# Turning the inverse's first matrices on VectorE instead of TensorE, with GpSimd taking a copy and half a low part per head turn

## The chip, the core and the metric

The kernel runs on one core of a Trainium2 chip. The metric is the device time of one execution in microseconds; lower is better. The core's engines run at the same time and meet only at semaphores: PE (TensorE) multiplies and loads weights, DVE (VectorE), ACT (ScalarE) and POOL (GpSimd) work elementwise, SP issues the loads from memory.

## What is computed

Two transformer blocks over 256 tokens of width 1024. The second holds a hybrid mixer of 8 heads: an HGRN2 part and a gated delta rule part. Cut to what the change touches:

```python
def gated_delta_chunked(q, k, v, beta, g):
    gam = jnp.cumsum(g, axis=-1)
    Lmat = jnp.exp(jnp.where(incl, gam[..., :, None] - gam[..., None, :], -jnp.inf))
    kb = k * beta[..., None]
    A = jnp.where(strict, jnp.einsum('bhntk,bhnsk->bhnts', kb, k) * Lmat, 0.0)
    T = lax.linalg.triangular_solve(eye + A, eye, left_side=True, lower=True, unit_diagonal=True)
    u = jnp.matmul(T, v * beta[..., None])
    w = jnp.matmul(T, kb * jnp.exp(gam)[..., None])
    ...
```

T is the inverse of a unit lower triangular matrix. The kernel builds it by doubling: the inverses of the 2x2 diagonal blocks, then of 4x4, and so on up to 128x128. It needs each intermediate both as it is (`yi`, `yc`) and turned (`xi`, `xc`).

## The kernel before

All projections go through weight chunks of 128x2048 numbers (1 MB). A ring of three slots holds each chunk three times: as loaded (`w_raw`), its rounded high part (`w_hi`, written by ACT in `split`), and the rest, the low part (`w_lo`, written by DVE: `w_low`, `w_low_half`, both through `low_of`, L1241). PE multiplies the high and the low parts (L2102 to L2109, L2114, L2121). SP loads the next chunk into a slot once its low part is written (`slot_free` waits on `lo_ready`).

The stage in question is a loop over the heads: `head(0)`, then seven turns of a loop, then `head(GH)`. Turn i does the projections of head i (24 quarters, six chunks) and, spread between them, the scans and the inverse of head i-1. Each engine's order is written out by hand, in its own `head`; semaphores tie them together. The loop's last six turns repeat one another.

At the end of a turn, for the head just projected:

- DVE writes unit matrices into `yi` (L1977, four 128x128 matrices side by side), later the first level: `nt` is the scaled negative of A (L2004), and a masked copy (L2007) puts its entries next to the diagonal into `yi`. A drain then raises `y0_ready`.
- PE, between quarters 21 and 22, turns the four matrices of `yi` through the unit matrix (L3004) into PSUM and raises `t_done`.
- ACT copies them to `xi` (L1193, `t_ready`) and two quadrants into `xc` (L1195).
- DVE meanwhile writes the low part of the next turn's first chunk in two halves (L1241), then scans (L2014), writes `hk` (L2015, `qk_ready`), takes the differences of the first two scan levels (`middle(1)`, `middle(2)`: L1796, `dd_ready`), `mt` (L2020), the scores (L2024, `lt2_ready`), empties a projection (L2028), and writes the gated output's low part (`delta_out_low`, L1740, `ogl_ready`).

At the start of the next turn PE asks in order for `t_ready`, `ntc_ready` and `lt2_ready` (first product of level 1, `inv_z(1)`, L2849), for the first chunk's low part (L2798), for `ogl_ready` (`inv_w(1)`, L2867), and for `xx_ready` (`inv_z(2)`, L2849 again). DVE gives `xx_ready` with a masked copy (`inverse(1)`, L1840) behind four small products (L1810, L1811) and one half of a low part.

Before the change POOL builds masks at the start, writes one whole low part (L631) and is otherwise idle.

Of the kernel before, what the change touches and what calls it, by code (L numbers as in the profile page):

```python
# [83 lines left out]
def emit(nc, ctx, a, out):  # L84
# [3 lines left out]
    def sem(name):  # L88
        return ctx.enter_context(nc.semaphore(name))
# [189 lines left out]
    def quad(ap, side):  # L279
        return ap[HD * side:HD * side + HD, :, :, HD * side:HD * side + HD].rearrange("p i e c -> p (i e) c")  # L280

    def kept(ap, side):
        return ap[HD * side:HD * side + HD, :, :, :].rearrange("p i e c -> p (i e) c")
# [4 lines left out]
    def yh_bank(tile):  # L288
        if tile < 4:
# [15 lines left out]
    w_loaded = [sem(f"w_loaded{s}") for s in range(RING)]  # L305
    slot_passed = sem("slot_passed")
    waited = sem("waited")
# [44 lines left out]
                         "gbc_ready", "gam_done", "lt_pre", "lt_ready"))  # L352
    qk_done, y0_ready, t_done, t_ready, ffn_step = (
        sem(n) for n in ("qk_done", "y0_ready", "t_done", "t_ready", "ffn_step"))
    zz_done, zc_ready, ww_done, wt_done, xx_ready, yy_ready, yt_done, xc_ready, ntc_ready = (
# [5 lines left out]
        sem(n) for n in ("gsq_ready", "gss_done", "grs_ready", "ogh_ready", "ogl_ready"))  # L361

    gate_tanh = sem("gate_tanh")
    ohh_ready, ohl_ready, ym_ready, ymh_ready, yml_ready = (
# [33 lines left out]
    def _(sp):  # L398
        def slot_free(c):
            if isinstance(c, int) and c < RING:  # L400
                return
            sp.wait_ge(lo_ready, c - RING + 1)
            sp.sem_inc(slot_passed, 1)

# [164 lines left out]
    def _(pool):  # L569
# [55 lines left out]
        for l in range(LEVELS):  # L625
# [5 lines left out]
        nc.gpsimd.tensor_tensor(w_lo[:, slot, :], w_raw[:, slot, :], w_hi[:, slot, :].bitcast(F32), ALU.subtract  # L631
                                ).then_inc(lo_ready, 1)

    BUILT_ID = 3
# [5 lines left out]
    def _(act):  # L640
# [303 lines left out]
        def head(i, gemm, main):  # L944
# [241 lines left out]
            if gemm:  # L1186
                act.wait_ge(y0_ready, i + 1)
                for side in range(2):
                    ins = nc.scalar.activation(kept(ntc, side), quad(nt, side), ACT.Copy)
                ins.then_inc(ntc_ready, 1)  # L1190
                act.wait_ge(t_done, i + 1)
                x0 = M[:, 5, :].rearrange("p (i e c) -> p i e c", i=TT, e=2)
                nc.scalar.activation(xi, x0, ACT.Copy).then_inc(t_ready, 1)  # L1193
                for side in range(2):
                    ins = nc.scalar.activation(kept(xc, side), quad(x0, side), ACT.Copy)  # L1195
                ins.then_inc(xc_ready, 1)
                level_exp(1, i + 1)
                level_exp(2, i + 1)
                nc.scalar.activation(n21, nt[:, :, :, HD:P], ACT.Copy)
# [34 lines left out]
    def _(dve):  # L1234
# [532 lines left out]
        def head(i, gemm, main):  # L1767
# [19 lines left out]
            def middle(l):  # L1787
                if l > 2 and not main:
                    return
                if l == 8:  # L1790
                    v.tensor_tensor(dd[:, 0, 0:P], hb[:, 0:P], hb[:, P - 1:P].to_broadcast([P, P]), ALU.subtract
                                    ).then_inc(dd_ready, 1)
                    return
                sz = 1 << (l - 1)
                blocks = hb.rearrange("p (n s) -> p n s", s=2 * sz)
                v.tensor_tensor(dd[:, l % 2, :].rearrange("p (n s) -> p n s", s=2 * sz), blocks,  # L1796
                                blocks[:, :, sz - 1:sz].to_broadcast([P, P // sz, 2 * sz]), ALU.subtract).then_inc(dd_ready, 1)

# [176 lines left out]
            if gemm:  # L1975
                key_lengths()
                v.tensor_copy(yi, ident[:].unsqueeze(1).unsqueeze(1).to_broadcast([P, TT, 2, P]))  # L1977
            w_low_j(2)
# [16 lines left out]
            if gemm:  # L1995
# [6 lines left out]
                for e in range(2):  # L2002
                    for b in range(TT):
                        v.scalar_tensor_tensor(out=nt[:, b, e, :], in0=kk[:, 2 * b, :], scalar=nbst[:, b, e:e + 1],  # L2004
                                               in1=lt[:, e, 2 * P * b:2 * P * b + P], op0=ALU.mult, op1=ALU.mult)
                settle()
                v.copy_predicated(yi, lmask[:, 0, :].bitcast(I32).unsqueeze(1).unsqueeze(1).to_broadcast([P, TT, 2, P]), nt)  # L2007
                v.drain().then_inc(y0_ready, 1)
                if main:
                    w_low_half(c0 + 3 + RING, 0, i, 6)  # L2010
                    w_low_half(c0 + 3 + RING, 1, i, 6)
                dve.wait_ge(lnf_ready, i + 1)
# [14 lines left out]
                dve.wait_ge(tok_done, i + 1)  # L2027
                v.tensor_copy(tok[:, 0, :], G[:, 1, :]).then_inc(evac[1], 1)  # L2028
                if main:
                    delta_out_low(i)  # L2030
                else:
                    w_low(c0 + 3 + RING, i, 6)
            settle()
# [61 lines left out]
    def _(pe):  # L2095
# [662 lines left out]
        def head(i, gemm, main):  # L2758
# [239 lines left out]
            quarter(21)  # L2998
            if gemm:
                pe.wait_ge(y0_ready, i + 1)  # L3000
                for b in range(TT):
                    for e in range(2):
                        at = T * b + P * e
                        ins = nc.tensor.transpose(M[:, 5, at:at + P], yi[:, b, e, :], ident[:])  # L3004
                ins.then_inc(t_done, 1)
            quarter(22)
# [81 lines left out]
```

## Time and profile before

| | |
|---|---|
| median of 3 runs | 1360.8 us (1360.49 to 1361.06) |
| the profiled execution | 1361.01 us, of which the trace's span is 1359.3 us |
| PE, share of the span busy | 99% |
| PE weight loads | 89% |
| DVE | 77% |
| ACT | 59% |
| POOL | 2% |
| granted TensorE clock, mean | 0.999 |
| one of the six like turns of the head loop | 49.26 us |

A row of a timeline gives the start of an instruction (or of a run of like ones), how long it took, its engine, line, operation and tiles, and in brackets how long the engine was idle before it and what released it, where that shows. Consecutive instructions overlap: the distance from start to start is what one costs its engine, and the duration is somewhat longer. Nearly all small tiles lie in one buffer and are called `arena`.

### The profile page before, as it was taken

How to read it: one execution, taken by the hardware profiler on the slowest of the kernel's cores; microseconds unless marked ns; L12 is line 12 of the kernel's file. 1: busy time of each engine (PE TensorE's matmuls, PEld its weight loads, DVE VectorE, ACT ScalarE, POOL GpSimd, SP SyncE). 2: the span in 40 equal slices, each digit the busy share in tenths (PEclk: the TensorE clock that was granted, in tenths of full speed). 3: DMA queues.
4: the chain of work that ended last, by engine and by line, in shares of the span. 5: the costliest groups of instructions: out<-in, count | busy, mean ns of one | idle time of the engine just before them, and what ended most of it. 6: DMA issues, size and time to landing. Idle time of an engine off the chain costs nothing.

```text
span 1359.3 us, 24392 instructions
## 1 busy us (share of the span) xinstructions
PE 1345.3 (99%) x8590; PEld 1208.7 (89%) x8590; DVE 1043.2 (77%) x1644; ACT 797.4 (59%) x1352; POOL 28.9 (2%) x72
## 2 busy tenths in 40 slices
PE   8999999999999999999999999999999999999998
PEld 7888888989888888888899999999999998988887
DVE  5798888777666686666778898888898877666665
ACT  4445555644344364444668898898898853544444
POOL 6000000000000010000000000000000000000000
PEclk9999999999999999999999999999999999999999
DMA  8565545655555756666574444554544286566661
GB/s 267 155 195 156 157 124 173 200 194 198 186 186 191 230 150 203 186 185 186 155 187 133 132 125 129 139 147 114 147 131 123 87 211 203 173 206 198 192 186 62
DMA packets 291215, 227.80 MB, mean 168 GB/s; under 512 B 10883, under 2 KB 270165, under 8 KB 291157
## 3 DMA queue, kind: packets, MB, share of 16 engines
q1 hardware_dynamic: 291012, 226.75, 56.2%
q8 instruction: 38, 0.62, 0.2%
q10 hardware_dynamic: 144, 0.26, 0.1%
q14 instruction: 21, 0.16, 0.0%
HBM read 225.90 MB, written 1.08 MB: 167 GB/s over the span
## 4 chain that ended last, share of the span: by engine, by line
PE 93%; DVE 3%; ACT 2%; issue 1%; DVEq 0%; ACTq 0%; DMA 0%
PE G L2114 11%; PE M L2114 10%; PE M L2107 7%; PE M L2108 7%; PE M L2109 7%; PE G L2121 6%; PE G L2102 5%; PE M L2121 5%; PE G L2104 5%; PE G L2103 5%; PE G L2264 2%; PE M L2867 1%; PE M L2849 1%; PE G L2107 1%; PE G L2109 1%; PE G L2108 1%
## 5 line engine op out<-in xcount | busy, mean ns | idle before, releaser
L1241 DVE TENSOR_TENSOR w_lo<-w_raw,w_hi 128x2048 fp32r<-128x2048 f32 (+2 forms) x247 | 477.7, 1942 | 122.1 <-ACT w_hi L655 114.9
L655 ACT ACTIVATE w_hi<-w_raw 128x2048 fp32r<-128x2048 f32 x197 | 375.9, 1909 | 171.4 <-PE M L2121 35.2
L2102 PE MATMUL G<-xa,w_hi 128*128 128x256 f32 x592 | 176.9, 299 | 0.0
L2104 PE MATMUL G<-xa,w_lo 128*128 128x256 f32 x592 | 167.2, 283 | 0.0
L2103 PE MATMUL G<-xa,w_hi 128*128 128x256 f32 x592 | 167.0, 282 | 0.0
L2114 PE MATMUL M<-xa,w_hi 128*128 128x512 f32 x600 | 147.9, 391 | 0.0
L2114 PE MATMUL G<-xa,w_hi 128*128 128x512 f32 x568 | 141.2, 392 | 0.0
L2114 PEld LDWEIGHTS M<-xa,w_hi 128*128 128x128 f32 x600 | 111.4, 188 | 23.0
L2114 PEld LDWEIGHTS G<-xa,w_hi 128*128 128x128 f32 x568 | 104.5, 188 | 21.0 <-issue 0.5
L2107 PE MATMUL M<-w_hi,xb 128*128 128x512 f32 x300 | 117.1, 390 | 0.1
L2108 PE MATMUL M<-w_lo,xb 128*128 128x512 f32 x300 | 116.9, 390 | 0.0
L2109 PE MATMUL M<-w_hi,xb 128*128 128x512 f32 x300 | 116.7, 389 | 0.0
L2102 PEld LDWEIGHTS G<-xa,w_hi 128*128 128x128 f32 x592 | 112.9, 191 | 1.4 <-issue 1.3
L2103 PEld LDWEIGHTS G<-xa,w_hi 128*128 128x128 f32 x592 | 112.9, 191 | 0.0
L2104 PEld LDWEIGHTS G<-xa,w_lo 128*128 128x128 f32 x592 | 112.6, 190 | 0.0
L882 ACT ACTIVATE arena<-arena 128x256 f32<-128x256 f32 x38 | 15.9, 418 | 137.4 <-DVE arena L1658 137.4
L2121 PE MATMUL M<-xa,w_lo 128*128 128x256 f32 x600 | 83.6, 284 | 0.0
L2121 PEld LDWEIGHTS G<-xa,w_lo 128*128 128x128 f32 x568 | 75.7, 191 | 3.8
L2121 PE MATMUL G<-xa,w_lo 128*128 128x256 f32 x568 | 78.4, 282 | 0.0
L2121 PEld LDWEIGHTS M<-xa,w_lo 128*128 128x128 f32 x600 | 76.9, 192 | 0.3
L2109 PEld LDWEIGHTS M<-w_hi,xb 128*128 128x128 f32 x300 | 56.3, 188 | 11.9
L2107 PEld LDWEIGHTS M<-w_hi,xb 128*128 128x128 f32 x300 | 56.4, 188 | 11.7 <-issue 0.4
(467 smaller groups left out, 2537.7 us busy)
## 6 DMA issues: line engine op xcount, KB each, us to landing
w_raw<-in_w_in SPq DMA_DIRECT2D x150, 512.0 KB, 4.9
w_raw<-in_ffn_w_in SPq DMA_DIRECT2D x88, 512.0 KB, 5.0
w_raw<-in_w_ff SPq DMA_DIRECT2D x64, 512.0 KB, 4.2
w_raw<-in_ffn_w_out SPq DMA_DIRECT2D x44, 512.0 KB, 4.9
w_raw<-in_w_in SPq DMA_DIRECT2D x33, 256.0 KB, 3.2
w_raw<-in_w_out SPq DMA_DIRECT2D x16, 512.0 KB, 3.8
w_raw<-in_w_branch_gdn SPq DMA_DIRECT2D x16, 512.0 KB, 5.3
w_raw<-in_w_branch SPq DMA_DIRECT2D x12, 512.0 KB, 4.5
```

The lines of the kernel that those rows point to most:

```text
L655: nc.scalar.activation(w_hi[:, slot, :], w_raw[:, slot, :], ACT.Copy).then_inc(hi_ready, 1)
L882: nc.scalar.activation(ffn_s[:, n, :], ffn_s[:, n, :], ACT.Silu).then_inc(ffr_ready, 1)
L1241: return v.tensor_tensor(dst, src, hi.bitcast(F32), ALU.subtract)
L2102: mm(out_, w[0], x[0], start=first, stop=False)
L2103: mm(out_, w[0], x[1], start=False, stop=False)
L2104: return mm(out_, w[1], x[0], start=False, stop=last_)
L2107: mm(out_, x[0], w[0], start=first, stop=False)
L2108: mm(out_, x[0], w[1], start=False, stop=False)
L2109: return mm(out_, x[1], w[0], start=False, stop=last_)
L2114: ins = mm(bank.rearrange("p (h t) -> p h t", h=2), wh[:, k, :], x[:, :, k, :], start=first and k == 0, stop=last_ and k == n - 1, skip_gr ...
L2121: ins = mm(bank[:, 0:T], wl[:, k, :], x[:, 0, k, :], start=first and k == 0, stop=last_ and k == n - 1, skip_group_check=first)
L2264: ins = mm(G[:, j, CW * i:CW * i + CW], x[:, k, P * i:P * i + P], w[j][:, k, :], start=first and k == 0, stop=last and k == KT - 1)
```

## The change

DVE turns the first matrices itself: `v.transpose` turns each 32x32 block of `yi` in its place and writes `xi`. At this level `yi` holds entries only in the 2x2 blocks on the diagonal, so this is the whole matrix turned. PE's four turns and `t_done` go, and so does ACT's copy from PSUM; ACT's quadrant copies read `xi`.

In the loop, the unit matrices are written by POOL, after `vn1_done` (the last product that reads the old `yi`), and DVE waits for them (`yi_ready`) ahead of its masked copy. POOL writes the first half of the low part of the next turn's first chunk, after `hi_ready` and `qk_ready`. DVE writes the second half, now behind L2028 and a wait for POOL's half (`pool_low`), and only this raises `lo_ready`. In `head(0)` it replaces a whole low part at that place. The differences of scan levels 1 and 2 become a scalar_tensor_tensor with the same two tensor inputs. SP's semaphore for passed slots is merged with another.

```diff
@@ gpsimd @@
+        c = FIRST["heads"] + 3 + RING
+        slot = c % RING
+        def first_half_low():
+            part = slice(0, CHUNK // 2)
+            nc.gpsimd.tensor_tensor(w_lo[:, slot, part], w_raw[:, slot, part], w_hi[:, slot, part].bitcast(F32), ALU.subtract
+                                    ).then_inc(pool_low, 1)
+        pool.wait_ge(hi_ready, c + 1)
+        pool.wait_ge(qk_ready, 1)
+        first_half_low()
+        with pool.Fori(1, GH) as i:
+            pool.wait_ge(vn1_done, i)
+            pool.sem_inc(waited, 1)
+            nc.gpsimd.tensor_copy(yi, ident[:].unsqueeze(1).unsqueeze(1).to_broadcast([P, TT, 2, P])).then_inc(yi_ready, 1)
+            pool.wait_ge(hi_ready, c + 1 + i * 6)
+            pool.wait_ge(qk_ready, i + 1)
+            pool.sem_inc(waited, 1)
+            first_half_low()
@@ scalar @@
-                act.wait_ge(t_done, i + 1)
-                x0 = M[:, 5, :].rearrange("p (i e c) -> p i e c", i=TT, e=2)
-                nc.scalar.activation(xi, x0, ACT.Copy).then_inc(t_ready, 1)
+                act.wait_ge(t_ready, i + 1)
                 for side in range(2):
-                    ins = nc.scalar.activation(kept(xc, side), quad(x0, side), ACT.Copy)
+                    ins = nc.scalar.activation(kept(xc, side), quad(xi, side), ACT.Copy)
@@ vector @@
+                if l <= 2:
+                    v.scalar_tensor_tensor(out=out_, in0=blocks, scalar=1.0, in1=middles, op0=ALU.mult, op1=ALU.subtract
+                                           ).then_inc(dd_ready, 1)
+                    return
+                v.tensor_tensor(out_, blocks, middles, ALU.subtract).then_inc(dd_ready, 1)
...
-                v.tensor_copy(yi, ident[:].unsqueeze(1).unsqueeze(1).to_broadcast([P, TT, 2, P]))
+                if not main:
+                    v.tensor_copy(yi, ident[:].unsqueeze(1).unsqueeze(1).to_broadcast([P, TT, 2, P]))
...
+                if main:
+                    dve.wait_ge(yi_ready, i)
+                    dve.sem_inc(waited, 1)
                 v.copy_predicated(yi, lmask[:, 0, :].bitcast(I32).unsqueeze(1).unsqueeze(1).to_broadcast([P, TT, 2, P]), nt)
                 v.drain().then_inc(y0_ready, 1)
-                if main:
-                    w_low_half(c0 + 3 + RING, 0, i, 6)
-                    w_low_half(c0 + 3 + RING, 1, i, 6)
+                v.transpose(xi.rearrange("p i e c -> p (i e c)"), yi.rearrange("p i e c -> p (i e c)")).then_inc(t_ready, 1)
...
                 v.tensor_copy(tok[:, 0, :], G[:, 1, :]).then_inc(evac[1], 1)
+                dve.wait_ge(pool_low, i + 1)
+                w_low_half(c0 + 3 + RING, 1, i, 6)
                 if main:
                     delta_out_low(i)
-                else:
-                    w_low(c0 + 3 + RING, i, 6)
@@ tensor @@
-            if gemm:
-                pe.wait_ge(y0_ready, i + 1)
-                for b in range(TT):
-                    for e in range(2):
-                        at = T * b + P * e
-                        ins = nc.tensor.transpose(M[:, 5, at:at + P], yi[:, b, e, :], ident[:])
-                ins.then_inc(t_done, 1)
```

How DVE's instructions stand at the end of a loop turn, before. `M` and `G` are the two PSUM tensors, `xb` holds the gated output.

```order
552 L2007 COPY_PREDICATED arena<-masks,arena 128x512
553 L1252 REGISTER_ALU
554 L1241 TENSOR_TENSOR w_lo<-w_raw,w_hi 128x1024 [waits hi_ready] x2
555 L2014 SCALAR_TENSOR_TENSOR arena<-ones,arena 128x128 [waits lnf_ready]
556 L2014 SCALAR_TENSOR_TENSOR arena<-ones,arena 128x128
558 L2015 SCALAR_TENSOR_TENSOR arena<-arena 128x256
559 L1796 TENSOR_TENSOR arena<-arena 128x256 x2
560 L2020 TENSOR_TENSOR arena<-M,arena 128x256
561 L2024 SCALAR_TENSOR_TENSOR arena<-M,arena 128x384 [waits qk_done]
563 L2028 COPY arena<-G 128x512 [waits tok_done]
566 L1740 SCALAR_TENSOR_TENSOR xb<-M,arena,xb 128x512
```

And the same stretch of the changed kernel, whose line numbers are higher by 18 to 27:

```order
552 L2034 COPY_PREDICATED arena<-masks,arena 128x512 [waits yi_ready]
553 L2036 STREAM_TRANSPOSE arena<-arena 128x512
554 L2039 SCALAR_TENSOR_TENSOR arena<-ones,arena 128x128 [waits lnf_ready]
557 L2040 SCALAR_TENSOR_TENSOR arena<-arena 128x256
558 L1817 SCALAR_TENSOR_TENSOR arena<-arena 128x256 x2
559 L2045 TENSOR_TENSOR arena<-M,arena 128x256
560 L2049 SCALAR_TENSOR_TENSOR arena<-M,arena 128x384 [waits qk_done]
562 L2053 COPY arena<-G 128x512 [waits tok_done]
563 L1270 REGISTER_ALU [waits pool_low]
564 L1259 TENSOR_TENSOR w_lo<-w_raw,w_hi 128x1024 [waits hi_ready]
567 L1758 SCALAR_TENSOR_TENSOR xb<-M,arena,xb 128x512
```

The two halves of the low part ahead of the scan have become one transposition; one half stands behind L2053 now, ahead of L1758.

PE's instructions between quarters 21 and 22 in the loop, before:

```order
2293 L2108 MATMUL G<-w_lo,xa 128x512
2294 L2109 MATMUL G<-w_hi,xa 128x512
2295 L3004 MATMUL M<-ident,arena 128x128 [waits y0_ready]
2296 L3004 MATMUL M<-ident,arena 128x128 x3
2297 L2107 MATMUL M<-w_hi,xa 128x512
```

And now:

```order
2291 L2133 MATMUL G<-w_lo,xa 128x512
2292 L2134 MATMUL G<-w_hi,xa 128x512
2293 L2132 MATMUL M<-w_hi,xa 128x512
2294 L2133 MATMUL M<-w_lo,xa 128x512
```

The four turns and their wait for `y0_ready` have gone; the two quarters follow each other directly.

## Rows read from the trace of the kernel before

**Rows 1.** The page: busy time and share of the span by engine.

```profile
PE 1345.3 (99%) x8590; PEld 1208.7 (89%) x8590; DVE 1043.2 (77%) x1644; ACT 797.4 (59%) x1352; POOL 28.9 (2%) x72
```

**Rows 2.** Timeline of PE at a turn's end: start, duration, engine, line.

```profile
813.90 0.39 PE L2109 MATMUL G<-w_hi,xa 128*128 128x512 f32 x1
814.13 0.60 PE L3004 MATMUL M<-ident,arena 128*128 128x128 f32 x4
...
814.80 0.39 PE L2108 MATMUL M<-w_lo,xa 128*128 128x512 f32 x1
```

**Rows 3.** Timeline of PE and its weight loads, the next turn's start (L2849 twice).

```profile
817.32 0.62 PE L2849 MATMUL M<-arena 128*128 128x128 f32 x4
...
818.95 0.64 PE L2798 MATMUL G<-xa,w_lo 128*128 128x256 f32 x4
...
821.63 0.54 PEld L2849 LDWEIGHTS M<-arena 128*128 128x128 f32 x4
821.74 0.62 PE L2849 MATMUL M<-arena 128*128 128x128 f32 x4
```

**Rows 4.** Timeline of DVE over the same boundary.

```profile
810.44 0.74 DVE L2007 COPY_PREDICATED arena<-masks,arena 128x512 f32<-128x512 int32 x1
811.38 2.36 DVE L1241 TENSOR_TENSOR w_lo<-w_raw,w_hi 128x1024 fp32r<-128x1024 f32 x2 [0.20 <-issue]
813.66 0.73 DVE L2014 TENSOR_TENSOR_SCAN arena<-ones,arena 128x128 f32<-128x128 f32 x2
814.31 0.46 DVE L2015 SCALAR_TENSOR_TENSOR arena<-arena 128x256 f32<-128x256 f32 x1
814.86 0.76 DVE L1796 TENSOR_TENSOR arena<-arena 128x256 f32<-128x256 f32 x2
816.04 1.02 DVE L2024 SCALAR_TENSOR_TENSOR arena<-M,arena 128x384 f32<-128x384 f32 x2
816.98 0.68 DVE L2028 COPY arena<-G 128x512 f32<-128x512 f32 x1
817.57 0.74 DVE L1740 SCALAR_TENSOR_TENSOR xb<-M,arena,xb 128x512 f32 x1
820.83 0.74 DVE L1840 COPY_PREDICATED arena<-masks,M 128x256 f32<-128x256 int32 x1
```

**Rows 5.** Timelines of ACT and SP over the same boundary.

```profile
811.24 0.60 ACT L1173 ACTIVATE arena<-arena 128x256 f32<-128x256 f32 x1 [0.21 <-issue]
...
828.48 1.90 ACT L655 ACTIVATE w_hi<-w_raw 128x2048 fp32r<-128x2048 f32 x1
```

```profile
813.99 0.37 SPq L413 DMA_DIRECT2D w_raw<-in_w_in  x1
```

**Rows 6.** Timelines of DVE and POOL while POOL writes its one low part.

```profile
480.49 1.23 DVE L1690 TENSOR_TENSOR arena<-res,arena 128x1024 f32<-128x1024 f32 x1
481.63 0.68 DVE L1493 SCALAR_TENSOR_TENSOR res<-res,M 128x512 f32<-128x512 f32 x1
485.84 0.89 DVE L1500 SCALAR_TENSOR_TENSOR arena<-res,stat,arena 128x512 f32<-128x512 f32 x1
490.62 0.75 DVE L1609 SCALAR_TENSOR_TENSOR arena<-res,stat,arena 128x512 f32<-128x512 f32 x1 [0.54 <-ACT stat L864]
```

```profile
480.61 5.57 POOL L631 TENSOR_TENSOR w_lo<-w_raw,w_hi 128x2048 fp32r<-128x2048 f32 x1 [454.40 <-ACT w_hi L655]
```

**Rows 7.** Timelines of POOL and DVE while the masks are built.

```profile
18.33 2.17 POOL L622 TENSOR_SCALAR_AFFINE_SELECT masks<-masks 128x64 f32<-128x64 f32 x1
23.84 0.24 POOL L622 TENSOR_SCALAR_AFFINE_SELECT masks<-masks 128x64 f32<-128x64 f32 x1
```

```profile
18.01 2.37 DVE L1241 TENSOR_TENSOR w_lo<-w_raw,w_hi 128x2048 fp32r<-128x2048 f32 x1 [0.68 <-ACT w_hi L655]
```

**Rows 8.** Timelines of PE and DVE at the first boundary and the last.

```profile
720.12 0.75 PE L2798 MATMUL G<-xa,w_lo 128*128 128x256 f32 x4 [0.54 <-DVE w_lo L1241]
```

```profile
1066.72 0.74 DVE L1840 COPY_PREDICATED arena<-masks,M 128x256 f32<-128x256 int32 x1 [0.36 <-PE M L2867]
```

More of the change, by code:

```diff
@@ L305, in emit @@
     w_loaded = [sem(f"w_loaded{s}") for s in range(RING)]
-    slot_passed = sem("slot_passed")
     waited = sem("waited")
@@ L352, in emit @@
                          "gbc_ready", "gam_done", "lt_pre", "lt_ready"))
-    qk_done, y0_ready, t_done, t_ready, ffn_step = (
-        sem(n) for n in ("qk_done", "y0_ready", "t_done", "t_ready", "ffn_step"))
+    qk_done, y0_ready, t_ready, ffn_step = (
+        sem(n) for n in ("qk_done", "y0_ready", "t_ready", "ffn_step"))
     zz_done, zc_ready, ww_done, wt_done, xx_ready, yy_ready, yt_done, xc_ready, ntc_ready = (
@@ L361, in emit @@
         sem(n) for n in ("gsq_ready", "gss_done", "grs_ready", "ogh_ready", "ogl_ready"))
+    yi_ready, pool_low = sem("yi_ready"), sem("pool_low")
     gate_tanh = sem("gate_tanh")
@@ L402, in slot_free @@
             sp.wait_ge(lo_ready, c - RING + 1)
-            sp.sem_inc(slot_passed, 1)
+            sp.sem_inc(waited, 1)
         def load_cols(c, slot, w, col):
@@ L1795, in middle @@
                 blocks = hb.rearrange("p (n s) -> p n s", s=2 * sz)
-                v.tensor_tensor(dd[:, l % 2, :].rearrange("p (n s) -> p n s", s=2 * sz), blocks,
-                                blocks[:, :, sz - 1:sz].to_broadcast([P, P // sz, 2 * sz]), ALU.subtract).then_inc(dd_ready, 1)
+                out_ = dd[:, l % 2, :].rearrange("p (n s) -> p n s", s=2 * sz)
+                middles = blocks[:, :, sz - 1:sz].to_broadcast([P, P // sz, 2 * sz])
+                if l <= 2:
[3 more added lines that the diff above has]
+                v.tensor_tensor(out_, blocks, middles, ALU.subtract).then_inc(dd_ready, 1)
             def decayed(l):
```

## The prediction

> **What bounds the kernel now.** I read the page first. PE is busy 99% of the span [rows 1], so time is gained only where PE has less to do, and only as far as nobody makes PE wait afterwards. Then I read PE's timeline at the end of a head turn, where the removed work stands [rows 2], and at the start of the next [rows 3], where PE asks for what the end of the turn made. PE waits for nobody at the six like boundaries. The question is how closely the others are behind it, so the third view is DVE's timeline over the same boundary [rows 4].
>
> It shows that DVE is a second bound here. Its masked copy L1840, which releases PE's second L2849, ends at 820.83 + 0.74 = 821.57, and PE's weight load for that product starts at 821.63, with no gap behind the load before it [rows 3, 4]. Taking 0.02 us for the signal, I put the slack at 0.04 us (an estimate; 0.06 at most). From L2007 to L1840 DVE has next to no idle time that anyone else causes, so whatever lengthens its row from L2007 to L1840 lengthens the turn, and PE can come earlier only by as much as DVE does plus 0.04.
>
> **The change part by part.** All per like turn, by the clock of [rows 2 to 4].
>
> PE. Without L3004 the start to start distances from L2109 on would be 0.23 each. From L2109 at 813.90 to the second product behind the turns at 814.80 they take 0.90 instead of 0.45 [rows 2], so L3004 costs PE 0.45 us. Over eight boundaries that is 3.6 us. It is the most that the steady part can bring.
>
> DVE up to the scan. L2007 gets a wait and a semaphore step ahead of it. What such a pair costs behind a drain is bounded by nothing and by L1241's 0.20 of idle before it, which no other engine causes [rows 4]. I take 0.14, nearer to that row: L2007 at 810.58, end 811.32, the transposition at 811.41. The trace has no DVE transposition. The bounds are L2028's start to start distance of 0.59 for 128x512 [rows 4] and twice that, if it went at half the rate. I take 0.60, since one pass over the same number of elements is what the row shows: end of its slot 812.01. The scan also needs L1173, which ends at 811.84 [rows 5], and so starts at 812.02 instead of 813.66: 1.64 earlier. That DVE no longer writes the unit matrices buys nothing here, because between them and L2007 it waits for ACT's exponential, behind ACT's own queue. POOL can write them as soon as PE has read the old ones, some 10 us ahead of L2007; this is their cover.
>
> DVE behind the scan. L2015 ends 1.11 behind the scan's start, at 813.13. From the scan's start to L2028 it was 816.98 - 813.66 = 3.32. The two differences as scalar_tensor_tensor cost about 0.06 more each (estimate, from 0.46 for L2015 against a half of 0.76 and the overlap), so L2028 starts at 812.02 + 3.44 = 815.46 and its slot ends at 816.06. Then the half low part takes 1.14 (half of 813.66 - 811.38), and L1740 starts at 817.20, where it was 817.57. DVE is 0.37 earlier at L1840, and with the slack of 0.04 PE can use 0.41 of its 0.45.
>
> This holds if POOL's half is ready by 816.06. POOL's whole low part took 5.57, but DVE's L1690 ran until 481.72, during the first 1.1 of it [rows 6]; the rest is 4.5, so a half is 2.25. It starts some 0.15 behind L2015's end, at 813.28, and is ready at 815.6 if nothing holds it. So there is 0.4 us of cover. The Trainium skill (GPSIMD Engine Reference, Performance versus the Vector engine) gives 4497 ns for such an operation of 2048 elements; by the row the trace agrees, and the sum is the same.
>
> The low part and SP. `lo_ready` of the next turn's first chunk comes at about 817.3 instead of 813.7. PE asks for it at its L2798, 0.45 before 818.95 [rows 3], and stays clear by 1.2. SP's load into that slot, issued at 813.99, goes out 3.5 later; ACT wants the chunk at 828.48 [rows 5], so 11 us are left of 14.5. I cost this at nothing; beyond 11 us of landing time each further tenth would be ACT's, and behind it PE's.
>
> ACT loses L1193 (0.5 us a turn). It was not late at these boundaries: nothing for the time. `lt2_ready` came with L2024's end at 817.06, 0.12 ahead of PE's load; it now comes 1.5 earlier and so follows PE's 0.45.
>
> The sum. Six like boundaries by 0.41 is 2.5. At the first one PE waited 0.54 for the low part [rows 8]; there DVE writes half a low part fewer (1.1), but the transposition now stands between L2007 and the scan, which L1173 had released before, and costs 0.2, and POOL's half must be waited for: 0.5 gained. At the last one DVE waited 0.36 for PE [rows 8], so PE's 0.4 comes through. In all 2.5 + 0.5 + 0.4 = 3.4. Against the profiled execution: 1361.0 - 3.4 = 1357.6; it stands 0.2 above the median, so 1357.4 for the median. The price of a DVE row that is longer than I take is six times the excess: a transposition at half rate (0.6) would cost 3.6, the whole gain.
>
> **The rivals.**
>
> *POOL queues behind the two differences.* [Rows 6] and [rows 7] show that POOL stands still while DVE reads two tensors from SBUF: the mask row that takes 0.24 alone took 2.17 beside L1241, until this ended. The two differences read two tensors from SBUF, start 0.09 behind L2015's end and end 0.97 behind it. If they come first and both pass, POOL runs from 814.1 to 816.4, DVE starts its half at 816.45, L1740 stands at 817.59, and nothing is left of the 0.37. Six boundaries bring 0, the first and the last 0.8: 1360.0. For it speaks that DVE needs no signal to go on, and POOL does; against it, that [rows 6] hold no pair of such DVE operations in a row.
>
> *DVE is held by POOL, and the kernel is slower.* If POOL gets in ahead of one of the two differences, DVE could stand still for what remains of 2.25 us. In [rows 6] L1500, with two SBUF inputs, starts 0.34 before POOL's end and takes 0.89, where its like L1609 takes 0.75: it lost 0.14, while L1493 with one input in PSUM lost nothing. So such an operation is held or slowed by a POOL already under way, and only the end of that is seen. Held in full, the differences end near 816.4, L2024 near 818.0, where PE's load would have been at 816.73, and L1740 starts at 819.6: 2.0 late, and the turn becomes 2.0 longer. Six of them, 1.5 at the first and 0.7 at the last, make 14: 1375. If the two share, and DVE loses 0.14 of each 0.34, or up to three quarters of its rate, the differences take 0.5 to 1.4 longer; beyond 0.41 each tenth costs 0.6 over the six, which gives 1361 to 1366. The point from which it decides is a delay of 0.41 us between L2015 and L2028.
>
> The Trainium skill (SBUF — State Buffer, Who interferes with whom) says that a VectorE instruction with two SBUF inputs contends with a GpSimd instruction that reads SBUF, and that the second one to start blocks until the first is done. By that rule the operation's name makes no difference, and the case of 1375 follows whenever POOL has asked before the second difference starts. The rows bear the rule out for a DVE that is first; for a POOL that is first they show only the 0.14.
>
> *The change doesn't take the work off.* The order shows the turns gone from PE, so this can only mean that another wait, `yi_ready` or the transposition's own length, fills DVE's row: 1361 to 1364.
>
> **How the numbers follow.** The forecast, with DVE passing almost unhindered: 0.42, and within it 1356.8 to 1359, of which about 0.3 lies more than 0.2% below 1360.8 (below 1358.1). POOL behind both: 0.23, at 1359 to 1361.5. Sharing: 0.10, at 1361 to 1366. Held: 0.20, near 1375. Another filler of DVE's row: 0.05. About 0.2% is what a measurement of this kernel can tell from no change. Faster: 0.31. Same: 0.12 + 0.20 + 0.03 + 0.02 = 0.37. Slower: 0.20 + 0.12 = 0.32. The range leaves out the held case and a little: 1356.5 to 1367.
>
> **What would show it.** Right: no L3004; the distance of L2849 from turn to turn 48.85 instead of 49.26; DVE's differences at about 0.48 each; POOL's half at 2.3; no idle time of DVE ahead of the half low part behind L2053. POOL behind both: POOL's half at 3.0 or more, DVE idle 0.3 or more there. Held: a difference of 2 us or more, PE waiting for L2049 (`lt2_ready`) and for the masked copy of `inverse(1)`. Wrong in the sum: a transposition of over 0.7, or DVE's row up to L2034 moved by more than 0.2. The prediction fails as a whole if DVE is not what follows PE closest at these boundaries, since then the 0.45 comes through undivided, or none does.

## The result and the profile after

The changed kernel takes 1374.62 us in the median of five runs (1373.15 to 1376.23), against 1360.8 before, which is the median of five runs too (1360.49 to 1361.06): 1.010 times as long, with a 95% interval of 1.0088 to 1.0111. Its profiled execution spans 1372.9 us, where that of before spans 1359.3: 13.6 us more. The forecast was 1357.4 with a range up to 1367.0, so the kernel became slower where a small gain was forecast, and the time lies outside the range. It lies within 0.4 us of the rival in which DVE is held by POOL.

The page of the changed kernel: the span, and each engine's busy time with its share (answers [rows 1]).

```profile
span 1372.9 us, 24388 instructions
PE 1346.0 (98%) x8558; PEld 1207.5 (88%) x8558; DVE 1055.9 (77%) x1638; ACT 794.0 (58%) x1344; POOL 54.6 (4%) x87
```

PE has 32 matmuls fewer and is 98% busy instead of 99%: the span has grown and the work has not. DVE shows 12.7 us more busy time with six instructions fewer. An instruction that stands still is counted as busy (the rows below show one), so this is the first sign of it.

DVE's timeline at one of the six like boundaries (start, duration, engine, line, what it writes and reads, count; the idle time before it in brackets). It is the boundary after the one of [rows 4].

```profile
864.27 1.13 DVE L2028 SCALAR_TENSOR_TENSOR arena<-M,arena 128x128 f32<-128x128 f32 x4
865.59 0.75 DVE L2034 COPY_PREDICATED arena<-masks,arena 128x512 f32<-128x512 int32 x1 [0.18 <-issue]
866.46 0.71 DVE L2036 STREAM_TRANSPOSE arena<-arena 128x512 f32<-128x512 f32 x1
867.09 0.70 DVE L2039 TENSOR_TENSOR_SCAN arena<-ones,arena 128x128 f32<-128x128 f32 x2
867.71 0.46 DVE L2040 SCALAR_TENSOR_TENSOR arena<-arena 128x256 f32<-128x256 f32 x1
868.26 2.98 DVE L1817 SCALAR_TENSOR_TENSOR arena<-arena 128x256 f32<-128x256 f32 x2
871.17 0.41 DVE L2045 TENSOR_TENSOR arena<-M,arena 128x256 f32<-128x256 f32 x1
871.66 1.02 DVE L2049 SCALAR_TENSOR_TENSOR arena<-M,arena 128x384 f32<-128x384 f32 x2
872.59 0.68 DVE L2053 COPY arena<-G 128x512 f32<-128x512 f32 x1
873.19 1.22 DVE L1259 TENSOR_TENSOR w_lo<-w_raw,w_hi 128x1024 fp32r<-128x1024 f32 x1
874.33 0.74 DVE L1758 SCALAR_TENSOR_TENSOR xb<-M,arena,xb 128x512 f32 x1
...
877.59 0.72 DVE L1863 COPY_PREDICATED arena<-masks,M 128x256 f32<-128x256 int32 x1
```

The two differences, L1817, take 2.98 where L1796 took 0.76 [rows 4]. Every other row is as long as its counterpart. A narrower stretch of the same timeline shows the first difference alone, and the list of the line sums up all sixteen:

```profile
868.26 0.43 DVE L1817 SCALAR_TENSOR_TENSOR arena<-arena 128x256 f32<-128x256 f32 x1
```

```profile
L1817 DVE SCALAR_TENSOR_TENSOR arena<-arena x16: 424/1512/2640, 715.2 to 1072.3; 128x256 f32<-128x256 f32 x16
```

The columns of the last are shortest, median and longest in ns: the first difference of a pair passes in 0.42 to 0.43, the second takes up to 2.64. POOL's timeline shows what runs beside it:

```profile
855.90 0.61 POOL L648 COPY arena<-ident 128x512 f32<-128x512 f32 x1 [35.88 <-PE M L2974]
868.35 2.62 POOL L639 TENSOR_TENSOR w_lo<-w_raw,w_hi 128x1024 fp32r<-128x1024 f32 x1 [11.83 <-DVE arena L2040]
```

POOL's half starts 0.09 behind the first difference and ends at 870.97; the pair ends at 871.24. And PE now waits, which it did not in [rows 3]. Its timeline at this boundary, and its waits by releaser from the first boundary to the last (us in total, times, longest):

```profile
872.83 0.69 PE L2874 MATMUL M<-arena 128*128 128x128 f32 x4 [0.78 <-DVE arena L2049]
...
878.36 0.72 PE L2874 MATMUL M<-arena 128*128 128x128 f32 x4 [0.83 <-DVE arena L1863]
```

```profile
PE M L2874 <- DVE arena L2049: 8.4, 8, 3.0
PE M L2874 <- DVE arena L1863: 5.2, 7, 0.9
PE G L2684 <- DVE w_lo L1259: 0.7, 1, 0.7
```

Where the 13.6 us come in is read by setting the first inverse product of each head side by side in the two traces. At the second boundary it starts at 770.94 instead of 768.04, 2.9 later; from there to the last boundary six turns take 50.92 each instead of 49.26 (1076.48 - 770.94 and 1063.61 - 768.04, by six), which adds 10.0; behind the last one come 0.7 more. By the page PE is idle for 26.9 us instead of 14.0, 12.9 more, and busy for 0.7 more, although 3.6 of its work went away: the products that are left took some 4 us more. Part of that is the first boundary, under a lower clock (last section); how the rest is spread stays open.

### The profile page after: what moved, and what is told of

The parts are those of the page before. It is cut to its first block, busy times and chain, and to the rows that moved or that the text cites. A ratio compares the mean times of both kernels' runs of the same rounds, so it can differ in the third digit from the quotient of the medians.

```text
span 1372.9 us, 24388 instructions
## 1 busy us (share of the span) xinstructions
PE 1346.0 (98%) x8558; PEld 1207.5 (88%) x8558; DVE 1055.9 (77%) x1638; ACT 794.0 (58%) x1344; POOL 54.6 (4%) x87
## 4 chain that ended last, share of the span: by engine, by line
PE 85%; DVE 6%; DVEq 3%; ACT 3%; issue 1%; ACTq 1%; DMA 0%
PE G L2139 11%; PE M L2139 9%; PE M L2132 7%; PE M L2133 7%; PE M L2134 7%; PE G L2146 6%; PE M L2146 5%; PE G L2127 5%; PE G L2129 5%; PE G L2128 5%; DVEq L1256 3%; PE G L2289 2%; PE M L2874 1%; PE M L2892 1%; DVE w_lo L1259 1%
## 5 line engine op out<-in xcount | busy, mean ns | idle before, releaser
L1259 DVE TENSOR_TENSOR w_lo<-w_raw,w_hi 128x2048 fp32r<-128x2048 f32 (+2 forms) x240 | 468.5, 1957 | 120.7 <-ACT w_hi L675 114.9
```

Source lines behind the costliest of these rows:

```text
L1259: return v.tensor_tensor(dst, src, hi.bitcast(F32), ALU.subtract)
```

## The experiments

In each turn of every kernel below the same stretch of DVE can be measured: from the start of the four products L2028 (before: L2004, at 809.24) to the start of L1758 (before: L1740). Before it was 817.57 - 809.24 = 8.33 us. It is given as **DVE's stretch**, beside the **turn** (mean of the six like ones), and both are put together behind the experiments.

**Which of the changed parts holds the differences?** Three kernels ran on one chip, on which the kernel before took 1360.85. First comes the form of the differences, which the changed kernel has as scalar_tensor_tensor:

```diff
-                if l <= 2:
+                if l <= 0:
```

> The changed kernel with the two differences as tensor_tensor, as before the change. Theory (what counts is the number of tensors read from SBUF, not the operation): the first is free, the second is held for some 2.3 us as now, and the time is 1374 to 1375, perhaps 0.5 lower since the first one is 0.06 shorter. Rival (scalar_tensor_tensor and tensor_tensor meet POOL differently): another length of the second difference, and with it a time more than 2 us away from 1374.6 either way.

It took 1374.62 us, 1.0097 times the time of before (1.0082 to 1.0113). The pair in its timeline:

```profile
869.72 2.98 DVE L1820 TENSOR_TENSOR arena<-arena 128x256 f32<-128x256 f32 x2
```

The pair is as long as in the changed kernel. The form makes no difference, neither held nor free (0.76 as tensor_tensor in [rows 4], 0.76 as scalar_tensor_tensor below).

Next, POOL works at the same point but reads nothing. It sets to zero its half of `w_lo`, and the half of `w_raw` that nobody reads any more. The kernel so leaves out half a low part per turn:

```diff
-            nc.gpsimd.tensor_tensor(w_lo[:, slot, part], w_raw[:, slot, part], w_hi[:, slot, part].bitcast(F32), ALU.subtract
-                                    ).then_inc(pool_low, 1)
+            nc.gpsimd.memset(w_raw[:, slot, part], 0.0).then_inc(pool_low, 1)
+            nc.gpsimd.memset(w_lo[:, slot, part].bitcast(F32), 0.0).then_inc(pool_low, 1)
...
-                dve.wait_ge(pool_low, i + 1)
+                dve.wait_ge(pool_low, 2 + i * 2)
```

> The changed kernel with POOL's half low part replaced by two memsets of the same 128x1024 shape, one of which sets that half of the low part to zero and one the half of w_raw that nobody reads any more: this leaves out half a low part per turn in the heads' stage. POOL is busy for some 2 us at the same place but reads nothing. Theory (POOL's reads hold DVE): the two differences take about 0.85 us together, and the time is that of my forecast, 1357.4 (1356.8 to 1359). Rival (any work of POOL's beside them holds DVE, or the hold is no port but the semaphore traffic): a second difference of 1.5 us or more and a time above 1366.

It took 1356.95 us, 0.9971 times before (0.9959 to 0.9983). DVE's and POOL's timelines:

```profile
860.63 0.76 DVE L1817 SCALAR_TENSOR_TENSOR arena<-arena 128x256 f32<-128x256 f32 x2
861.30 0.42 DVE L2045 TENSOR_TENSOR arena<-M,arena 128x256 f32<-128x256 f32 x1
```

```profile
860.68 0.96 POOL L639 MEMSET w_raw<- 128x1024 f32 x1 [11.81 <-DVE arena L2040]
861.57 0.96 POOL L640 MEMSET w_lo<- 128x1024 f32 x1
```

POOL is busy beside the differences from 0.05 behind the first one's start to beyond their end, and they pass at full speed. Neither POOL's being at work nor its writing holds DVE; what is left is its reading. This run is also the forecast's case without its flaw: turn 48.81, which is 49.26 less PE's 0.45.

Third, POOL starts only when both differences are through:

```diff
-        pool.wait_ge(qk_ready, 1)
+        pool.wait_ge(dd_ready, 2)
...
-            pool.wait_ge(qk_ready, i + 1)
+            pool.wait_ge(dd_ready, 2 + i * 8)
```

> The changed kernel, but POOL's half waits until DVE has finished both differences (dd_ready) instead of hk (qk_ready). Theory (a POOL operation that reads SBUF holds DVE's second difference, which also reads two tensors from SBUF, until it is done): the two differences take about 0.85 us together instead of 2.98, POOL's half about 2.3 instead of 2.6, DVE then waits about 0.4 us for it ahead of its own half, and the time falls from 1374.6 to about 1360 (1359 to 1361.5). Rival (the length comes from the new length of DVE's row, 0.7 us of transposition and the wait for the unit matrices, and from POOL's half as a term in the chain, wherever it stands): POOL's half begins 0.8 us later, so the turn gets longer still or stays, 1374 to 1379.

It took 1361.92 us, 1.0008 times before (0.9998 to 1.0017): no difference that this measurement can tell, and 0.4 above the range that was expected. POOL, then DVE:

```profile
863.40 2.41 POOL L639 TENSOR_TENSOR w_lo<-w_raw,w_hi 128x1024 fp32r<-128x1024 f32 x1 [12.68 <-DVE arena L1817]
```

```profile
862.46 0.76 DVE L1817 SCALAR_TENSOR_TENSOR arena<-arena 128x256 f32<-128x256 f32 x2
...
865.93 1.22 DVE L1259 TENSOR_TENSOR w_lo<-w_raw,w_hi 128x1024 fp32r<-128x1024 f32 x1 [0.68 <-POOL w_lo L639]
```

The hold is gone, and nearly 13 us with it. What is left is DVE's wait for POOL, 0.68 instead of the expected 0.4, and it eats the gain as that rival of the forecast had it. POOL's undisturbed half is 2.41, not 2.25; that and the start at 0.18 behind the pair put the turn at 49.50 instead of 49.26.

**Can the reading be moved to where DVE does not read two tensors from SBUF?** Behind the differences stand three steps that read PSUM (L2045 and L2049 have one input there and one in SBUF, the copy L2053 has its only input there). They go ahead of the differences:

```diff
-                if l <= 2:
+                if l <= 0:
...
-                middle(1)
-                middle(2)
...
                 v.tensor_copy(tok[:, 0, :], G[:, 1, :]).then_inc(evac[1], 1)
+                middle(1)
+                middle(2)
```

> The changed kernel in which DVE does mt, the scores and the emptying of the projection (L2045, L2049, L2053, each with one input in PSUM) directly behind hk, beside POOL's half, and then the two differences (as tensor_tensor) and its half of the low part. Theory (only two SBUF inputs meet POOL): L2045, L2049 and L2053 keep 0.42, 0.55 and 0.68 us, the first difference is held by 0.5 us at most, L1758 starts about 0.2 us earlier against PE than before the change, and the time is about 1358.5 (1357.5 to 1360). Rival (DVE is slowed by POOL whatever it reads): L2049 or L2053 of 1 us or more and a time above 1366. Rival (ACT wants the differences earlier and its level_exp holds DVE and PE in the next turn): the differences are short but the time is above 1361.

It took 1358.82 us, 0.9983 times before (0.9974 to 0.9992). DVE and POOL at the boundary:

```profile
861.29 0.42 DVE L2043 TENSOR_TENSOR arena<-M,arena 128x256 f32<-128x256 f32 x1
861.80 1.02 DVE L2047 SCALAR_TENSOR_TENSOR arena<-M,arena 128x384 f32<-128x384 f32 x2
862.74 0.68 DVE L2051 COPY arena<-G 128x512 f32<-128x512 f32 x1
863.34 1.08 DVE L1820 TENSOR_TENSOR arena<-arena 128x256 f32<-128x256 f32 x2
```

```profile
861.38 2.41 POOL L639 TENSOR_TENSOR w_lo<-w_raw,w_hi 128x1024 fp32r<-128x1024 f32 x1 [11.83 <-DVE arena L2040]
```

The three steps are as long beside POOL as without it, and POOL keeps its 2.41. POOL ends at 863.79, 0.45 into the pair, and the pair is 0.32 longer than the free one.

**What do the two halves of the change give alone?** First without POOL's half: DVE writes both halves at the old place, behind the transposition.

```diff
-        first_half_low()
...
+                if main:
+                    w_low_half(c0 + 3 + RING, 0, i, 6)
+                    w_low_half(c0 + 3 + RING, 1, i, 6)
                 dve.wait_ge(lnf_ready, i + 1)
...
-                dve.wait_ge(pool_low, i + 1)
-                w_low_half(c0 + 3 + RING, 1, i, 6)
```

> The changed kernel without POOL's half: DVE turns the matrices and then writes both halves of the low part where it did before the change; POOL still writes the unit matrices. PE is free of L3004's 0.45 a turn and nobody is held. Theory (DVE's row between its masked copy and inverse(1) is a second bound with 0.04 us of slack): the row grows by the transposition's slot (0.63) and by the wait for the unit matrices (0.18), so the turn is 0.75 longer than before, and the time about 1365.5 (1364 to 1367). Rival (PE alone bounds, and what it no longer does comes out as time when nobody is held): 1357 to 1358.

It took 1365.06 us where the kernel before took 1361.09 on that chip: 1.003 (1.0018 to 1.0042), slower. PE's work is less by the same 0.45 a turn, and it waits for the scores (L2045 in this kernel):

```profile
PE M L2870 <- DVE arena L2045: 6.7, 8, 0.9
```

The turn is 0.63 longer than before; 0.75 had been expected. So DVE is the second bound, as the forecast's first part has it: to take 0.45 from PE and put 0.64 on DVE's stretch lengthens the turn by 0.63.

Then POOL's half alone, with PE's turns and ACT's copy kept and the unit matrices written by DVE:

```diff
+            if gemm:
+                pe.wait_ge(y0_ready, i + 1)
+                for b in range(TT):
+                    for e in range(2):
+                        at = T * b + P * e
+                        ins = nc.tensor.transpose(M[:, 5, at:at + P], yi[:, b, e, :], ident[:])
+                ins.then_inc(t_done, 1)
...
-                v.transpose(xi.rearrange("p i e c -> p (i e c)"), yi.rearrange("p i e c -> p (i e c)")).then_inc(t_ready, 1)
```

> One part of the change alone: POOL's half of the low part with DVE's half behind it, and the differences as scalar_tensor_tensor; PE turns the matrices and ACT copies them as before the change, DVE writes the unit matrices. Theory (the loss is the hold of the second difference, 2.2 us a turn, which DVE's saved half, 1.14, doesn't pay for; it doesn't need the transposition): the differences take 2.98 as in the changed kernel; DVE's row is shorter than there by the transposition, of which the wait for ACT takes most, so the turn is 50.7 to 50.9 against 49.25 before and 50.94 changed, and the time about 1372.5 (1371 to 1374). Rival (the loss comes from the transposition's 0.63 in DVE's row as much as from POOL): a turn of 50.3 or less, 1370 or less.

It took 1373.88 us, 1.009 times the 1361.22 of before on that chip (1.0074 to 1.0105). The pair stands for 2.97, and the scan ahead of it now waits 0.68 for ACT's copy of PE's turned matrices:

```profile
866.73 0.74 DVE L2035 TENSOR_TENSOR_SCAN arena<-ones,arena 128x128 f32<-128x128 f32 x2 [0.68 <-ACT arena L1191]
...
867.95 2.97 DVE L1817 SCALAR_TENSOR_TENSOR arena<-arena 128x256 f32<-128x256 f32 x2
```

```profile
868.03 2.61 POOL L640 TENSOR_TENSOR w_lo<-w_raw,w_hi 128x1024 fp32r<-128x1024 f32 x1 [48.17 <-DVE arena L2036]
```

The loss needs neither the transposition nor POOL's unit matrices.

**Is the hold as long as what remains of POOL's instruction?** POOL takes a quarter (512 columns), DVE the other three:

```diff
-            part = slice(0, CHUNK // 2)
+            part = slice(0, CHUNK // 4)
...
-                w_low_half(c0 + 3 + RING, 1, i, 6)
+                w_low_rest(c0 + 3 + RING, i, 6)
```

> The changed kernel with POOL's part cut from 1024 to 512 columns and DVE's part grown from 1024 to 1536. Theory (the second difference is held until POOL's operation ends, however long it is): POOL's part takes about 1.5 us, the two differences about 1.85 together instead of 2.98, DVE's part 0.57 more; each turn is 0.5 to 0.6 shorter than in the changed kernel, and the time about 1371 (1370 to 1372.5). Rival (the hold is a fixed price of a meeting, a queue drained or a lock passed over): the differences keep 2.98, DVE's part adds 0.57 a turn, 1378.

It took 1369.2 us, 1.0061 times the 1361.09 of before (1.0046 to 1.0076), under the 1370 to 1372.5 that were expected. The six like turns give what had been counted (50.35 instead of 50.92, 3.4 in all). The first boundary had been left out, and it gives nearly as much: the next one's first product starts at 768.12 instead of 770.94. At the first boundary PE's wait is 1.1 shorter (1.96 instead of 3.04), and from its first product to its second it takes 5.15 instead of 5.98, with the clock at 1.00 throughout (last section).

```profile
865.21 1.86 DVE L1823 SCALAR_TENSOR_TENSOR arena<-arena 128x256 f32<-128x256 f32 x2
```

```profile
865.29 1.50 POOL L639 TENSOR_TENSOR w_lo<-w_raw,w_hi 128x512 fp32r<-128x512 f32 x1 [11.82 <-DVE arena L2046]
```

POOL is 1.12 shorter, and so is the pair (1.86 for 2.98).

**Can the rest of PE's 0.45 be had?** In the reordered kernel the turn was 49.06; PE still came up against the masked copy L1863 of `inverse(1)`, which stands behind a half low part of the next chunk. That chunk's low part is now cut into 512 and 1536 columns, the small part ahead of the masked copy:

```diff
+        def w_low_cut(base, h, i=0, step=0):
+            slot = base % RING
+            dve.wait_ge(hi_ready, base + i * step + 1)
+            part = slice(0, CHUNK // 4) if h == 0 else slice(CHUNK // 4, CHUNK)
...
-                w_low_half(c0 + 4 + RING - 6, 0, i, 6)
+                w_low_cut(c0 + 4 + RING - 6, 0, i, 6)
             inverse(1)
...
-                w_low_half(c0 + 4 + RING - 6, 1, i, 6)
+                w_low_cut(c0 + 4 + RING - 6, 1, i, 6)
```

> The reordered kernel (differences behind the emptying of the projection), and in it the second chunk's low part is cut into 512 and 1536 columns instead of two halves, with inverse(1) between them as before, so that the masked copy which releases PE's second product of the inverse comes up to 0.5 us earlier. Theory (that copy is what PE waits for, 0.15 us a turn, in the reordered kernel): the waits go, the turn falls from 49.05 to 48.9, and the time from 1358.8 to 1357.7 (1357.0 to 1358.5). Rival (the same row of DVE is late again one level further on, behind the larger part): no gain, 1358.5 to 1359.5, with PE waiting for the masked copy of inverse(2).

It took 1358.4 us, 0.998 times 1361.09 (0.9971 to 0.9989): nearly as the reordered one. The turn is 49.00. The second product of the inverse is now 4.43 behind the first, as where POOL only writes, and was 4.58 behind it in the reordered kernel. But the larger part holds up the masked copy of `inverse(2)`: the third product is 4.51 behind the second instead of 4.42, and the fourth 4.30 behind the third instead of 4.20. So the same cut for the third chunk around `inverse(2)`:

```diff
-                w_low_half(c0 + 5 + RING - 6, 0, i, 6)
+                w_low_cut(c0 + 5 + RING - 6, 0, i, 6)
             inverse(2)
...
-                w_low_half(c0 + 5 + RING - 6, 1, i, 6)
+                w_low_cut(c0 + 5 + RING - 6, 1, i, 6)
```

> The reordered kernel with both the second and the third chunk's low part cut into 512 and 1536 columns around inverse(1) and inverse(2). In the run before, PE's wait had moved from the second product of the inverse (0.15 us a turn) to the third (0.1), behind DVE's low part ahead of inverse(2). Theory (nothing else of DVE's follows PE closely): no wait of PE is left in the six like boundaries, the turn is 48.81 as where POOL only wrote, and the time is about 1357.5 (1357.0 to 1358.2). Rival (the larger parts behind make a later copy of DVE's late): the turn stays at 49.0, 1358 to 1359.

It took 1357.15 us, 0.9972 times the 1361.22 of before (0.996 to 0.9983), faster than the kernel before and than the changed one. The turn is 48.81, PE's whole 0.45. DVE at the two masked copies:

```profile
867.18 0.68 DVE L1259 TENSOR_TENSOR w_lo<-w_raw,w_hi 128x512 fp32r<-128x512 f32 x1
867.83 0.76 DVE L1871 COPY_PREDICATED arena<-masks,M 128x256 f32<-128x256 int32 x1
868.39 1.78 DVE L1259 TENSOR_TENSOR w_lo<-w_raw,w_hi 128x1536 fp32r<-128x1536 f32 x1
...
871.54 0.69 DVE L1259 TENSOR_TENSOR w_lo<-w_raw,w_hi 128x512 fp32r<-128x512 f32 x1 [0.16 <-issue]
872.25 0.74 DVE L1871 COPY_PREDICATED arena<-masks,M 128x256 f32<-128x256 int32 x1
```

**All turns by one number.** If DVE's stretch sets the turn and PE has 0.04 of room, as the forecast had it, then the turn is 49.26 + (stretch - 8.33) - 0.04, and never under 48.81, which is 49.26 without PE's 0.45 (with POOL's half alone, where PE keeps its turns, never under 49.26):

| kernel | DVE's stretch | turn by it | turn measured |
|---|---|---|---|
| before | 8.33 | | 49.26 |
| changed | 10.06 | 50.95 | 50.92 |
| differences as tensor_tensor | 10.04 | 50.93 | 50.93 |
| POOL's half alone | 9.90 | 50.79 | 50.80 |
| POOL a quarter | 9.45 | 50.34 | 50.35 |
| transposition alone | 8.97 | 49.86 | 49.89 |
| POOL behind both | 8.60 | 49.49 | 49.50 |
| reordered | 8.16 | 49.05 | 49.06 |
| POOL writes only | 7.83 | 48.81 | 48.81 |

None is off by more than 0.03, so nothing else is needed to explain these turns. The last two kernels are not in it, since there another part of DVE's row sets the turn, or none.

**And all holds by one more.** Free, the second difference starts 0.34 behind the first (0.76 less one of 0.42). From there to POOL's end it was 870.97 - 868.60 = 2.37 in the changed kernel, and the pair lost 2.98 - 0.76 = 2.22; with a quarter 1.24 and 1.10; with POOL's half alone 2.35 and 2.21; reordered, where the first of the pair is met, 0.45 and 0.32. The loss is each time 0.13 to 0.15 less than the overlap.

**One input is not always safe.** The unit matrices that POOL copies from `ident` (its row at 855.90 above) meet an instruction of DVE with a single input, in SBUF. Here it is in the kernel before, where POOL is idle, and in the changed one:

```profile
801.26 0.28 DVE L1972 TENSOR_SCALAR arena<-arena 128x256 f32<-128x256 f32 x1
```

```profile
856.29 0.36 DVE L1995 TENSOR_SCALAR arena<-arena 128x256 f32<-128x256 f32 x1
```

POOL ends at 856.51, 0.22 into it, and it is 0.08 longer: 0.14 less than the overlap once more. It takes 0.28 in the kernel with POOL's half alone, where DVE writes the unit matrices, and 0.36 to 0.38 in all seven turns of every kernel here in which POOL copies them. That it is held and not slowed is argued from this one length of overlap.

## Why the forecast was wrong

**The step that failed** is the weighing of the rivals, and in it one reading. The forecast took DVE to pass almost unhindered because in [rows 6] L1500 overlapped POOL's last 0.34 and lost only 0.14, and it allowed this to be a sharing at some part of the rate. By the holds above it is neither: of L1500's overlap 0.34 less 0.14, so 0.20, cost nothing, near the 0.13 to 0.15 that cost nothing in the other cases. L1500 fits a hold in full. Read so, what looks like a mild slowing was the end of a full stop, seen through an overlap hardly longer than the part that is free. An effect bounded by one short overlap cannot be scaled as a rate; two lengths are needed to tell a stop from a slowing.

**The second thing it rested on** was that POOL would come too late to be first: DVE needs no signal to go on. That is right for the first difference. For the second it is not enough: POOL starts 0.09 behind the first's start, 0.25 ahead of where the second would have started, and gets in between two DVE instructions that follow each other without a gap. The case "POOL queues behind both" treated the two as one. The condition that the other rival named, that POOL has asked before the second difference starts, could have been read from the forecast's own numbers: 813.28 for POOL, and a second difference at 0.34 behind 813.22. It stood in the text and was given 0.20. And the section on the chip has the engines meet only at semaphores; DVE and POOL also meet where both read SBUF.

The Trainium skill (SBUF — State Buffer, Who interferes with whom) states just this: with two SBUF inputs on VectorE and a reading GpSimd, the second to issue blocks until the first is done. All runs here agree: the operation's name does not matter (2.98 in both forms), a POOL that only writes does not hold the pair (0.76), and DVE's steps that read PSUM are not held (0.42, 1.02 and 0.68 beside POOL).

**The rival that came true**: its condition, its place, its sign and its price. It gave 1375, worked out from a turn 2.0 longer; the turn became 1.66 longer and the first boundary cost 2.5 instead of 1.5 (its second product at 725.65 instead of 723.10). The six turns came out smaller since the pair ends 0.27 behind POOL's end, where over 0.8 had been taken; the first boundary larger since there PE's wait for `lt2_ready` was 3.04 and part of the products behind it ran at the lower clock. That 1375 came so close is in part luck: the turns were taken 2.0 too high over the six, and the first boundary 1.4 too low (2.9 by the next one's first product).

**What held.** PE saves 0.45 a turn (48.81 where nothing hinders). DVE is the second bound, and the room is 0.04: the table. POOL's unit matrices came in time: its copy is 0.61 long and stands 9.7 us ahead of L2034. They cost DVE the 0.08 of L1995, which the turns don't show. The later `lo_ready` made no weight chunk late for ACT: in the six like turns none of its waits ends with a load. The bounds of the transposition held too.

**Terms that were mis-sized**, read where POOL only writes. From L2034's start to the scan it is 1.50 instead of 1.44: the transposition's slot is 0.63, not 0.60, and it lasts 0.71. The pair of wait and step costs 0.12 (865.59 - 864.27 = 1.32 against 1.20 before), not 0.14. The differences as scalar_tensor_tensor cost nothing more, not 0.12: scan to L2053 is 3.28, not 3.44. In all DVE's stretch is 0.50 shorter, not 0.37, so PE could have used all of its 0.45. The first boundary gained 0.94 there (its second product at 722.16 instead of 723.10), not 0.5. POOL's half is 2.41, not 2.25. The forecast halved the 4.5 of the whole low part, but the length does not go by the columns alone: with 512 columns less it is 1.12 shorter (2.62 and 1.50, both beside a difference), which would make 2.24 of the 2.41 for 1024 and leaves 0.17 that does not shrink (an estimate).

**"POOL behind both"** was given as 1360.0 and measured as 1361.9. The mechanism was right; the half's 0.16 and the start 0.18 behind the pair make a wait of 0.68, larger than the gain.

The sum for a kernel without the hold was nearly right, at 1357.4 against 1356.95 where POOL only writes. The price of each step in the rows of DVE and POOL was within 0.16 of what it measured; the choice between cases was what missed.

## What to carry to other kernels

Before a GpSimd operation that reads SBUF is laid beside a row of VectorE, look at each VectorE instruction that starts while it runs: those with two SBUF inputs stood until it ended, also directly behind another, and one with a single SBUF input was longer too. Put there steps that read PSUM, or let GpSimd only write; both passed at full speed here. When the first and second bound are 0.04 us apart, work taken from the first counts only as far as the second's row gets shorter too; measure that row from one fixed point to another, and the turn follows to within 0.03. And a slowing seen in one short overlap may be the end of a full stop.

## What was not expected of the hardware

After the longest wait of PE, 3.04 us at the first boundary, the granted clock fell. The first product there and the clock of the stretches behind it (busy us and count of PE, its weight loads, DVE, ACT and POOL, then PEclk, DMA share, GB/s):

```profile
719.67 1.20 PE L2874 MATMUL M<-arena 128*128 128x128 f32 x4 [3.04 <-DVE arena L2049]
```

```profile
717.00:722.00 5.00, 2.33 (x11) 2.36 (x12) 4.63 (x9) 2.98 (x11) 0.81 (x1) 0.75 0.00 0
722.00:727.00 5.00, 5.00 (x41) 5.00 (x41) 3.95 (x8) 3.46 (x7) 0.00 (x0) 0.91 0.92 252
727.00:732.00 5.00, 5.00 (x45) 5.00 (x44) 3.93 (x9) 2.20 (x9) 0.00 (x0) 1.00 0.77 223
```

The mean of 0.75 and then 0.91 lies between the two levels, 2.4 and 1.2 GHz, so part of each stretch ran at the lower one. The four products take 1.20 instead of 0.69 at the other boundaries. With the differences as tensor_tensor the same stretches read:

```profile
717.00:722.00 5.00, 2.16 (x10) 2.19 (x11) 4.63 (x8) 2.97 (x11) 0.98 (x1) 0.70 0.00 0
722.00:727.00 5.00, 5.00 (x30) 5.00 (x30) 2.87 (x7) 2.66 (x4) 0.00 (x0) 0.62 0.89 245
```

There PE is busy throughout the second stretch and gets 30 matmuls done instead of 41, and this execution took 1376.09 us where that kernel's fastest took 1373.44. In the kernel before the clock is 1.00 over the same stretches. The spread of the changed kernel is 3.1 us against 0.6 before, and the mean granted clock of its five executions goes with it: 0.999 at 1373.15 and 1373.42, 0.998 at 1374.62, 0.997 at 1374.88 and 0.996 at 1376.23. So the spread most likely comes from how long the lower clock lasts; where it fell in the other executions no trace shows. The other waits of PE at this boundary: 2.44 with POOL's half alone, where the two stretches read 0.77 and 0.89, and 1.96 with a quarter, where both read 1.00. The waits of 0.8 at the like boundaries leave the clock at 1.00.
